# The attention gate's projection as three single passes by head, with its weight rests on GpSimd and the gated sequence's two parts on VectorE

## What is computed

```python
h = rmsnorm_2(x, norm_g[l])
proj = h @ w_in[l]
q, k, v, ga, iq, ik, iw, xr, gr, ma, mb = jnp.split(proj, offsets, axis=-1)
...
attn = dsa_attention(q, k, v, iq, ik, iw).reshape(B, S, H * Dh)   # 8 heads of 128
y_a = (attn * jax.nn.silu(ga)) @ w_out_attn[l]
...
hr = rg_lru(xr, w_rg[l], b_rg[l], w_ig[l], b_ig[l], lru_lambda[l])
y_b = (hr * jax.nn.silu(gr)) @ w_out_rnn[l]
merged = jax.nn.sigmoid(ma) * y_a + jax.nn.sigmoid(mb) * y_b
x = x + merged @ w_o[l]
```

## Time and profile before

| what | us |
|---|---|
| median of 3 runs | 1933.44 (1932.25 to 1938.01) |
| the profiled execution: its own time | 1938.37 |
| its span | 1936.6 |
| TensorE busy | 1864.8 |
| VectorE busy | 833.4 |
| ScalarE busy | 671.3 |
| GpSimd busy | 269.4 |

### The profile page before, as it was taken

One profiled execution on the slowest core, in us unless ns is written; L12 is line 12 of the kernel. 1 busy time (PEld: TensorE's weight loads), 2 busy tenths in 40 slices (PEclk: granted clock), 3 DMA queues, 4 the chain that ended last, 5 costly groups with the idle time before them and its releaser, 6 DMA issues.

```text
span 1936.6 us, 28315 instructions
## 1 busy us (share of the span) xinstructions
PE 1864.8 (96%) x11306; PEld 1266.5 (65%) x11306; DVE 833.4 (43%) x1889; ACT 671.3 (35%) x1287; POOL 269.4 (14%) x239
## 2 busy tenths in 40 slices
PE   8999999999998999999999999999999999999998
PEld 7884444444446874444444445888989978888997
DVE  4764112112114763221111124557665655667656
ACT  4533111111113642111111112546755544575544
POOL 1400000000000400000000001873000057800000
PEclk8999999999998999999999999999999999999999
DMA  8378999999995468999999997453415754533353
GB/s 293 152 296 354 419 428 427 429 428 428 429 427 206 180 249 359 406 428 427 427 429 429 429 428 273 155 195 125 172 54 189 248 198 157 188 121 117 110 173 135
DMA packets 121430, 557.58 MB, mean 288 GB/s; under 512 B 5008, under 2 KB 49584, under 8 KB 96240
## 3 DMA queue, kind: packets, MB, share of 16 engines
q1 hardware_dynamic: 119696, 551.51, 71.5%
q10 hardware_dynamic: 1440, 4.36, 0.6%
q0 software_dynamic: 192, 0.30, 0.1%
HBM read 555.11 MB, written 1.05 MB: 287 GB/s over the span
## 4 chain that ended last, share of the span: by engine, by line
PE 57%; DVE 4%; DMA 3%; ACT 3%; issue 2%; POOL 0%; SPq 0%; POOLq 0%; DVEq 0%; ACTq 0%
PE bank L2315 7%; PE bank L2346 5%; PE bank L2464 3%; PE bank L2466 3%; PE bank L2465 3%; PE bank L2443 3%; PE bank L2444 3%; PE bank L2445 3%; DMA ring<-w_up_dram 3%; PE bank L2317 3%; PE bank L2550 3%; PE bank L2413 2%; PE bank L2038 2%; PE bank L2047 2%; PE bank L2480 1%
## 5 line engine op out<-in xcount | busy, mean ns | idle before, releaser
L2315 PE MATMUL bank<-ring,work 128*64 128x512 f32 x544 | 242.5, 601 | 9.3 <-issue 9.3
L1651 DVE TENSOR_TENSOR work<-work,bank 64x512 f32<-64x512 f32 x64 | 43.9, 685 | 439.5 <-ACT work L1000 439.4
L2317 PE MATMUL bank<-ring,work 128*64 128x512 f32 x512 | 228.9, 602 | 0.0
L776 POOL TENSOR_TENSOR stat<-stat,power 128x1 f32<-128x1 f32 (+1 forms) x18 | 10.8, 602 | 1501.7 <-DVE stat L1231 961.3
L816 POOL TENSOR_TENSOR w_lo<-ring,w_hi 128x512 fp32r<-128x512 f32 (+1 forms) x160 | 208.7, 1320 | 53.9 <-ACT w_hi L1050 50.9
L1000 ACT ACTIVATE work<-bank 64x512 f32<-64x512 f32 x64 | 37.9, 592 | 465.9 <-PE bank L2317 465.9
L1050 ACT CAST w_hi<-ring 128x512 fp32r<-128x512 f32 (+1 forms) x208 | 123.3, 606 | 121.6 <-PE bank L2466 81.5
L2346 PE MATMUL bank<-ring,work 128*64 128x512 f32 x480 | 155.8, 595 | 1.8 <-ACT work L1005 0.4
L2315 PEld LDWEIGHTS bank<-ring,work 128*64 128x64 f32 x544 | 73.1, 138 | 121.1 <-issue 119.2
L1869 DVE TENSOR_TENSOR w_lo<-ring,w_hi 128x512 fp32r<-128x512 f32 (+1 forms) x176 | 116.4, 678 | 79.0 <-ACT w_hi L1155 78.6
L1667 DVE SCALAR_TENSOR_TENSOR act_hi<-bank,stat,act_hi 128x512 fp32r<-128x512 f32 x64 | 48.1, 751 | 211.2 <-ACT act_hi L1010 211.2
(11 more groups left out here) (354 smaller groups left out, 4510.8 us busy)
## 6 DMA issues: line engine op xcount, KB each, us to landing
ring<-w_in_dram SPq DMA_DIRECT2D x34, 2048.0 KB, 8.7
ring<-w_gate_dram SPq DMA_DIRECT2D x34, 2048.0 KB, 20.9
ring<-w_up_dram SPq DMA_DIRECT2D x32, 2048.0 KB, 26.3
ring<-w_down_dram SPq DMA_DIRECT2D x30, 2048.0 KB, 25.8
ring_tail<-w_down_dram SPq DMA_DIRECT2D x18, 2048.0 KB, 23.7
work<-w_gate_dram SPq DMA_DIRECT2D x16, 2048.0 KB, 20.6
work<-w_up_dram SPq DMA_DIRECT2D x16, 2048.0 KB, 26.0
ring_tail<-w_up_dram SPq DMA_DIRECT2D x16, 2048.0 KB, 27.2
```

The source lines that it names most:

```text
L2315: pe.matmul(m_bank(m)[gate, :], lhs, wg[:, k], start=(k == 0), stop=(k == KD - 1), skip_group_check=True)
L2317: mu = pe.matmul(m_bank(m)[up, :], lhs, wu[:, k], start=(k == 0), stop=(k == KD - 1), skip_group_check=True)
```

## The change

1. The gate's two weight pieces enter `SPLIT` (`QGA`), with chunks of another form: chunk `2 * hh + half` holds the 128 columns of head hh for four of the eight row blocks. The second chunk of a head is closed by the gate's tile, the first by `chunk_used`.
2. TensorE's `gate(hh)` is three single passes for each of the eight row blocks, 24 matmuls of 128x256, and waits for `chunk_lo`, half by half.
3. ScalarE rounds the two chunks of a head in `round_gate`: of heads 0 and 1 ahead of the first exponentials and behind them, and of head hh + 2 at the end of head hh.
4. GpSimd takes the rests of these chunks, behind its other rests.
5. The gated sequence's rounding goes from ScalarE (heads 5 to 7) to VectorE, between `logits` and `weights` of heads 1, 3 and 5, and its rest to the same place at heads 2, 4 and 6.
6. The first four chunks of words for the pair products are rounded at heads 6 and 7 on ScalarE (before: 2 and 3), and their rests taken at heads 6 and 7 on VectorE (before: 3 and 4).

```diff
                  + [(PGR, ("gr", 3), KD * 512), (PGR + 1, ("gr", 7), KD * 512), (PGR + 2, ("gr", 10), KD * 384)]
+                 + [(PGA, ("ga", 3), KD * 512), (PGA + 1, ("ga", 7), KD * 512)]
...
-        QXR, QV, QGR, QPAIR = 5, 8, 10, 13
+        QXR, QV, QGR, QGA, QPAIR = 5, 8, 10, 13, 15
...
+        def closed_by(q, c):
+
+            if q in (QGA, QGA + 1):
+                return ("ga", 4 * (q - QGA) + c // 2) if c % 2 else None
+            return SPLIT[q][1] if c == chunks_of(q) - 1 else None
...
+        def gate_chunk(layer, hh, half):
+
+            return chunk(layer, QGA + hh // 4, 2 * (hh % 4) + half)
+
+        def by_k(t, g):
+
+            return t[:, g % CHUNKS].rearrange("p (k n) -> p k n", n=P)
+
+        def gate_words_of(w, hh, half):
+
+            return w[:, KD // 2 * half:KD // 2 * (half + 1), hh % 4 * P:(hh % 4 + 1) * P]
...
+                for hh in range(HEADS):
+                    w = arrive2(pool, layer, PGA + hh // 4)
+                    for half in range(2):
+                        g = gate_chunk(layer, hh, half)
+                        pool.wait_ge(chunk_hi, g + 1)
+                        pool.tensor_tensor(by_k(w_lo, g), gate_words_of(w, hh, half), by_k(w_hi, g), ALU.subtract
                                            ).then_inc(chunk_lo, 1)
...
+                def round_gate(hh):
+
+                    w = arrive2(act, layer, PGA + hh // 4)
+                    for half in range(2):
+                        g = gate_chunk(layer, hh, half)
+                        chunk_left(act, g - CHUNKS)
+                        act.copy(by_k(w_hi, g), gate_words_of(w, hh, half)).then_inc(chunk_hi, 1)
...
-                def round_hidden(part):
-
-                    act.wait_ge(rnn_gated, RT * (layer + 1))
-                    dst, src = ((ui_hi_rest[:], ui[:, KD:]), (act_hi[:, 0:CHUNKS], ui[:, 0:CHUNKS]),
-                                (act_hi[:, CHUNKS:], ui[:, CHUNKS:KD]))[part]
-                    act.copy(dst, src).then_inc(ui_hi_ready, 1)
...
+                round_gate(0)
                 for j in range(8, RT):
                     silu_gates(j)
                 exponentials2(0)
+                round_gate(1)
                 gate(0)
                 for hh in range(HEADS):
                     empty(("PT2", layer, hh), pT2[:, hh % 2], bank(("PT2", layer, hh))[:, 0:3 * P])
                     if hh + 1 < HEADS:
                         exponentials2(hh + 1)
                         gate(hh + 1)
-                    if 2 <= hh < 4:
-                        round_words(QPAIR, 2 * (hh - 2), 2 * (hh - 2) + 2)
-                    elif hh >= 5:
-                        round_hidden(hh - 5)
+                    if hh + 2 < HEADS:
+                        round_gate(hh + 2)
+                    else:
+                        round_words(QPAIR, 2 * (hh - 6), 2 * (hh - 6) + 2)
...
+                def round_hidden(part):
+
+                    dst, src = ((ui_hi_rest[:], ui[:, KD:]), (act_hi[:, 0:CHUNKS], ui[:, 0:CHUNKS]),
+                                (act_hi[:, CHUNKS:], ui[:, CHUNKS:KD]))[part]
+                    dve.wait_ge(rnn_gated, RT * (layer + 1))
+                    dve.tensor_copy(dst, src).then_inc(ui_hi_ready, 1)
...
                 for hh in range(HEADS):
                     if hh + 1 < HEADS:
                         logits(hh + 1)
+                        if 1 <= hh and hh % 2 == 1 and hh < 6:
+                            round_hidden(hh // 2)
+                        elif 2 <= hh and hh < 7:
+                            rest_of_hidden(hh // 2 - 1)
                         weights(hh + 1)
-                    if 3 <= hh < 5:
-                        rest_of_words(QPAIR, 2 * (hh - 3), 2 * (hh - 3) + 2)
+                    if hh >= 6:
+                        rest_of_words(QPAIR, 2 * (hh - 6), 2 * (hh - 6) + 2)
                     attended(hh)
-                    if hh >= 6:
-                        rest_of_hidden(hh - 6)
-                rest_of_hidden(2)
                 rest_of_words(QPAIR + 1)
...
                 def gate(hh):
                     name = ("ga", layer, hh)
-                    w_ = arrive2(pe, layer, PGA + hh // 4)
                     claim(name)
-                    done(by_feature(bank(name)[:, 0:SEQ], w_, hh % 4), name)
+                    dst = bank(name)[:, 0:SEQ]
+                    for half in range(2):
+                        g = gate_chunk(layer, hh, half)
+                        pe.wait_ge(chunk_lo, g + 1)
+                        for kk in range(KD // 2):
+                            k = KD // 2 * half + kk
+                            pe.matmul(dst, by_k(w_hi, g)[:, kk], hT_hi[:, k], start=(k == 0), stop=False)
+                            pe.matmul(dst, by_k(w_hi, g)[:, kk], hT_lo[:, k], start=False, stop=False)
+                            mm = pe.matmul(dst, by_k(w_lo, g)[:, kk], hT_hi[:, k], start=False, stop=(k == KD - 1))
+                        if half == 0:
+                            mm.then_inc(chunk_used, 1)
+                    done(mm, name)
```

More of the change, by code:

```diff
@@ L592, in chunks_of, with marked @@
             return KD if SPLIT[q][2] == KD * 384 else -(-SPLIT[q][2] // 512)
+        def closed_by(q, c):
+            if q in (QGA, QGA + 1):
+                return ("ga", 4 * (q - QGA) + c // 2) if c % 2 else None
+            return SPLIT[q][1] if c == chunks_of(q) - 1 else None
+        def marked(q, n):
+            return sum(closed_by(q, c) is None for c in range(n))
         CHUNK0 = [sum(chunks_of(z) for z in range(q)) for q in range(len(SPLIT) + 1)]
-        MARKED0 = [sum(chunks_of(z) - (SPLIT[z][1] is not None) for z in range(q)) for q in range(len(SPLIT) + 1)]
+        MARKED0 = [sum(marked(z, chunks_of(z)) for z in range(q)) for q in range(len(SPLIT) + 1)]
         def chunk(layer, q, c):
@@ L604, in chunk_left @@
             q = next(z for z in range(len(SPLIT)) if r < CHUNK0[z + 1])
-            c, tile = r - CHUNK0[q], SPLIT[q][1]
-            if tile is not None and c == chunks_of(q) - 1:
+            c = r - CHUNK0[q]
+            tile = closed_by(q, c)
+            if tile is not None:
                 full(eng, (tile[0], layer, tile[1]))
             else:
-                eng.wait_ge(chunk_used, layer * MARKED0[-1] + MARKED0[q] + c + 1)
+                eng.wait_ge(chunk_used, layer * MARKED0[-1] + MARKED0[q] + marked(q, c + 1))
+        def gate_chunk(layer, hh, half):
[4 more added lines that the diff above has]
+            return w[:, KD // 2 * half:KD // 2 * (half + 1), hh % 4 * P:(hh % 4 + 1) * P]
         def chunk_words(words, q, c):
@@ L816, in _ @@
                         pool.tensor_tensor(w_lo[:, g % CHUNKS, 0:n], w[:, k], w_hi[:, g % CHUNKS, 0:n], ALU.subtract
+                                           ).then_inc(chunk_lo, 1)
+                for hh in range(HEADS):
[4 more added lines that the diff above has]
+                        pool.tensor_tensor(by_k(w_lo, g), gate_words_of(w, hh, half), by_k(w_hi, g), ALU.subtract
                                            ).then_inc(chunk_lo, 1)
```

## The result

The changed kernel took 1947.41 us, the median of 6 runs (1943.80 to 1954.49). The kernel before took 1934.99 us beside it (6 runs, 1932.25 to 1938.01). The ratio is 1.0068, with a 95% interval of 1.0056 to 1.0080: slower by 10.8 to 15.5 us. Forecast were 1947.4 us.

What follows compares the result with a forecast made beforehand. TensorE alone was taken to set the steady heads' pace. Per layer 3.4 + 2.55 + 0.15 + 0.9 = 7.0 us, two layers 14.0 us, on a median of 1933.44 gave 1947.4 us; range 1939 to 1955.

Steps and rivals of the forecast that it cites:

- Are the operands there?: Steady heads: each gate's preparation waits for the gate before; 2.72 + 2.88 = 5.60 us period against 5.09, +2.55 us a layer.
- The heads' start: First heads up to gate 2: gating products contend with GpSimd, gate 2 starts at 15.9 us against 11.89, +3.4 us a layer.
- The gated sequence on VectorE: Rounding moved between `logits` and `weights`: costs nothing, hidden by the next gate and scores; uncovered, up to 1.4 us a head.
- The heads' end: Ahead of the last `PT2` copy: gate 7's copy and two word casts delay it, +0.15 us a layer.
- Clock: TensorE nearly idle between gates 1 and 2: one likely clock fall a layer, 0.9 us, bounds 0 and 1.7.
- half the price: At gate 2: 0.9 us of a clock fall's 1.7 us charged, since part may lie in idle time.
- Sum: Both layers' heads: 7.0 us a layer, 14.0 us in all, giving a median of 1947.4 us.
- the uncontended start: Rival at the heads' start: GpSimd lets VectorE through and the clock stays; +7.6 us, 1941.0 us, chance 0.20.
- repeated falls: Rival in the heads: two more clock falls in each layer, full price for the first; +22.4 us, 1956 us, chance 0.15.
- the gate in time: Rival in the steady heads: gate operands arrive in time and the kernel gets faster, 1924 us at best, chance 0.07.
- break-even of 0.84 us: Steady-head loop: GpSimd's step must take 0.84 us or less, not 1.35, for the period to match 5.09 us.
- the forecast's choice: Heads' start: contended value taken, VectorE products at 1.53 us beside GpSimd against 0.37 undisturbed; +3.4 us a layer, not +1.1.

Runs made afterwards that it cites:

- half the rest: Changed kernel with GpSimd subtracting only 64 of each row block's 128 columns of the gate's weights: 1938.30 us, against 1935.11 for the kernel before.
- two ahead: Changed kernel with each gate rounded at the start of the head before, ahead of the copy that waits for TensorE: 1943.01 us, against 1935.11 before.
- logits first: Changed kernel with VectorE's gating products 3 to 10 moved behind `logits(1)`: 1945.11 us, against 1934.63 for the kernel before.
- the sequence back: Changed kernel with the gated sequence's roundings on ScalarE again and rests at the heads' end, as before the change: 1951.88 us, against 1935.11 before.
- caught up at head 1: Changed kernel, gating products 3 to 10 behind `logits(1)`, gates rounded one head further ahead from head 1 on: 1935.21 us, against 1935.24 before.
- the other run of the changed kernel: The changed kernel once more, unaltered, beside later runs: 1949.49 us, against 1934.63 for the kernel before, ratio 1.0045 to 1.0084.
- before with logits first: Kernel before the change, with only gating products 3 to 10 moved behind `logits(1)`: 1934.33 us, against 1935.24 unmoved.
- the catch-up at head 2: Changed kernel, gating products 3 to 10 behind `logits(1)`, `round_gate(4)` directly after `round_gate(3)`, behind gate 2's copy: 1939.29 us, against 1935.24 before.

## Why the prediction was right, point by point

- **Are the operands there?** They were not, by the order on ScalarE that the prediction read from the code. The preparation was 2.65 us where 2.72 were forecast (GpSimd's step 1.27 us instead of 1.35), the passes 2.95 us from the gate's first to the next operation where 2.88 were forecast (the first pass takes 0.20 us, the others 0.12). The two misses cancel: the period was 5.60 us, as forecast. In the first layer the period to gate 4 was 5.90 us, since GpSimd began 1.05 us behind the casts' start there and not 0.75; why is open. The run with half the rest shows that GpSimd's step is a term of it with its full length, the run with two ahead that the order on ScalarE is the cause.
- **The heads' start.** Gate 0 started 3.38 us behind the stage's start (3.3 forecast), `logits(1)` at 11.12 (11.1), gate 2 at 15.87 (15.9). The run with logits first shows that the gating products beside GpSimd were the path.
- **The gated sequence on VectorE.** (Its parts stand in the loop's passes 1 to 6, between `logits` and `weights` of heads 2 to 7, one head on from the numbers that the change's description gives.) Forecast at nothing, and it cost nothing; the undisturbed cast of 128x1024 takes 0.68 us, the one beside GpSimd 1.80, and the weights were still in time. The run with the sequence back shows it.
- **The heads' end.** +0.15 us a layer forecast, +0.09 measured (2.73 against 2.64).
- **Clock.** One fall with gate 2 behind it, as forecast: gate 2 took 4.44 us for 2.97. The cost was 1.5 us, not 0.9, so taking half the price was the wrong choice; it is within the stated bounds of 0 and 1.7. A second fall, at gate 0 of the first layer, wasn't forecast. It made gate 1 end at 11.52 us instead of 10.58, and cost nothing in the changed kernel, since gate 2 waited for VectorE; in the run that caught up at head 1 it decided. The steady heads stayed at 1.00 behind gate 2.
- **Sum.** By the parts, a layer's heads were forecast to take 7.0 us more, and took 7.89 and 7.63: 15.5 us for both and not 14.0, of which 1.2 are the clock's price and 0.3 the long period. From the stage's start, gate 2's end came at 20.31 us, 5.0 later (4.3 forecast with the clock), 4.99 in the second layer, and the five periods took 2.84 and 2.55 us more (2.55 forecast). The median rose by 12.4 us, in the other run of the changed kernel by 14.9, for 14.0 forecast. That 1947.4 us were forecast and 1947.41 measured is luck: the forecast stands on a median of 1933.44 us for the kernel before, which took 1934.99 beside the change, and this 1.55 us makes good for a difference of the medians 1.6 us too small.
- **Rivals.** The uncontended start is out by the 4.97 us of the gating products, repeated falls by the clock of the steady heads, and the gate in time by the waits for `w_lo`. Its break-even of 0.84 us for GpSimd's step was somewhat too high: the measured loop is 5.60 - 1.27 = 4.33 us and GpSimd's step, which meets 5.09 us at 0.76; at 0.72 us the period was 5.06 us. The reason for the forecast's choice, VectorE products with both operands in SBUF beside GpSimd's subtraction, is borne out by the runs two ahead, logits first, and before with logits first. With it goes the rule of the Trainium skill ("SBUF — State Buffer", Who interferes with whom) that stood beside it: the two products that met GpSimd took 1.54 and 1.49 us.

## What to carry to other kernels

When work is moved off the bound engine, first ask where its new preparation stands in the helper's queue: a cast behind a copy that waits for the bound engine makes a loop, and its period is the sum of the hand-overs, however short the passes become. Then ask what VectorE does in the same microseconds as a new GpSimd step, since here eight products went from 2.77 to 4.97 us that way. And a remedy is to be judged with what it moves next to what: getting ahead helped only where GpSimd's steps no longer met the path's VectorE work and the clock was kept through the first wait.

## What the hardware did that was not expected

- A VectorE `tensor_scalar` on only 128x2 elements takes 0.17 us alone and up to 1.29 us beside a GpSimd subtraction; the weights' `tensor_scalar` steps of 128x128 and 128x256 went from 0.29 and 0.35 to 1.40 and 1.36. How long it waits goes by what is left of the GpSimd step and not by its own size. The Trainium skill ("SBUF — State Buffer", Who interferes with whom) says that `tensor_scalar` can enter modes that use the shared ports and that the later one blocks for the whole instruction. The trace agrees: the step of 1.36 us began 0.06 us behind the start of a GpSimd step and ended 0.15 us behind its end. The one of 1.40 us is recorded 0.04 us ahead of GpSimd's and waited all the same, so within such margins the records don't tell which came first.
- Not everything on VectorE waits. Beside the same subtractions the maxima (`tensor_reduce`, 0.29 and 0.41 us) and the first step of `logits`, with one input in PSUM (0.55), took as long as in the kernel before.
- The scans slow down as well: six took 5.73 us beside two GpSimd steps and 3.59 us without.
- GpSimd mostly loses less, since the VectorE steps that it meets are shorter: two steps take 2.53 us undisturbed, 2.72 beside the eight products of the changed kernel and 3.02 beside the scans. But beside VectorE's rest of 128x768 (0.95 us) a single step took 2.09 us instead of 1.29, in the catch-up at head 2.
- The wait of 2.56 us ahead of gate 0 let the clock fall in one layer and not in the other of the same kernel (in the run that caught up at head 1: 1.00 in the first, 0.69 in the second). What decides it is open.
